# The last 16 of 256 tokens leave a dense expert product and are gathered instead

## The chip, the cores and the metric

The kernel runs on one core of a Trainium2 chip. The metric is the device time of one execution in microseconds. The engines are TensorE (PE; its loads of stationary operands are PEld), VectorE (DVE), ScalarE (ACT), GpSimd (POOL) and SyncE (SP), each with its own in-order queue of instructions; they wait for each other on semaphores.

## What is computed

Two transformer blocks over 256 tokens of width 1024. The change touches the last part only, a layer with 16384 experts (PEER), cut here to what matters:

```python
def peer(h, w_q, subkeys, w_down, w_up):            # h: 256 x 1024
    q = (h @ w_q)                                   # 8 heads, two halves of 128
    s = einsum('btphd,phnd->btphn', q, subkeys)     # 128 scores for each half
    v, i = top_k(s, 16)
    cand = v[..., 0, :, None] + v[..., 1, None, :]  # 16 x 16 pairs
    cidx = i[..., 0, :, None] * 128 + i[..., 1, None, :]
    tv, tj = top_k(cand, 16)                        # 16 experts a token and head
    eidx = take_along_axis(cidx, tj)
    w = softmax(tv)
    a = gelu(einsum('btd,btpkd->btpk', h, w_down[eidx]))
    return einsum('btpk,btpkd->btd', w * a, w_up[eidx])
```

So each token uses 128 of the 16384 rows of w_down.

## The kernel before

It does not gather. It computes the down products of all experts densely, multiplies their gelu by a matrix of routing weights that is zero where an expert is not chosen, and multiplies by w_up. The experts are cut into 128 tiles (NE) of 128 experts; expert number is i * 128 + j, a tile has one j. A tile is [128 experts x 256 tokens]; WA[:, j, :] holds it.

All weights come as one stream of pieces of 128 x 1024 float32 (512 KB), issued by SP into three ring slots. Each piece q is split into a high part of type fp32r by ScalarE (split_high, L192) and a low part, the remainder, by VectorE or GpSimd (split_low, L199), three pieces ahead of TensorE (AHEAD). The ring slot is free once the low part is made. A product of two such pairs is three matmuls, high-high, low-high, high-low (mm3, L273, L274, L277). In the wide form (down_wide, L2337 and L2341) the token operand's two parts lie side by side, so that a matmul of 512 columns does two of the three, one of 256 the third; ScalarE copies the right half out (L2355) and VectorE adds it (L2357).

The stage runs in this order.

Query pieces: 16 pieces, scores, and the top 16 of each half on VectorE (L2427 to L2434).

Lead tiles 0 to 35 (FIRST = 36), by lead_tile(u): the plain product, the split of the piece three ahead with the low part on GpSimd, the gelu on ScalarE (L2365). Beside them VectorE does the second top 16 (L2466 to L2473), the decoding of its places (to L2497), four picks of indices (L2510 to L2514, twice for each half of the tokens) and the softmax (L2516 to L2525; Exp on ScalarE, L2518, between tile 29 and 30). Tiles 6 to 29 are in a hardware loop (nc.Fori), the others are unrolled. Before tile 33, TensorE turns indices and weights (turn_route, L2532), before tile 35 come the first one-hot matrices.

64 steps g, one for each 4 tokens (TB, ROUTES): VectorE makes one-hot matrices of 4 tokens (onehots, L2557, L2558), ScalarE scales one by the weights (weights_in, L2566), TensorE multiplies them (route_product, L2575) and then does the wide tile 36 + g. The routing weights of these tokens go to WA by ScalarE's copy for tiles that have no gelu yet (route_copy, L2586) and by VectorE's multiplication for those that have (route_multiply, L2594). late_gelu (L2610, L2612) and late_weigh (L2623) weigh the part of the tile whose tokens' weights are already there. Each queue is in the written order: ScalarE in step g has weights_in(g+1), late_gelu(g-1), route_copy(g-1), the high part of the piece three ahead, the copy of the right half. VectorE has route_multiply(g-2), late_weigh(g-2), onehots(g+2), the low part, the addition.

Then 28 pairs of a wide down tile and an up tile (pair), then the remaining 100 up tiles (last_tile, last_up), and the end.

## Time and profile before

| | us |
|---|---|
| median of 3 runs | 1719.74 |
| lowest, highest | 1718.23, 1723.38 |
| span of the profiled execution | 1718.3 |
| TensorE busy | 1692.9 |
| VectorE busy | 1283.4 |
| ScalarE busy | 970.7 |
| GpSimd busy | 234.7 |

Times in the rows are in microseconds from the start of the span. A line of a timeline gives start, duration, engine, line, operation, output and input; several instructions that follow each other can be merged into one with a count. Durations of neighbouring instructions of one engine overlap, so the distance between starts is what one costs. The words in square brackets are the idle time of the engine before it and who ended it. "Share" of DMA is the mean busy share of the 16 DMA engines. PEclk is TensorE's granted clock as a share of 2.4 GHz.

In the execution profiled, the lead tiles take 943 to 1046 us in all, with the last query scores among the first three; the 64 steps run to 1281, the pairs to 1437, the up tiles to 1701.

### The profile page before, as it was taken

What the parts mean: (1) busy time and instruction counts of PE and PEld (TensorE: products, weight loads), DVE (VectorE), ACT (ScalarE), POOL (GpSimd) and SP (SyncE); (2) the same over time, 40 slices, a digit from 0 to 9 for tenths busy, and PEclk for the clock granted to TensorE, in tenths of its full rate; (3) what the DMA queues carried; (4) which work ended last, traced back from release to release, by engine and by line L of the source; (5) the groups of instructions that cost most, each with busy time, mean ns of one, the idle gap of its engine ahead of it and who ended that gap; (6) DMA issues with size and microseconds to landing.
All of it is one profiled execution on the core that took longest, in us unless ns stands there. A gap on an engine that the chain in (4) does not pass through costs nothing.

```text
span 1718.3 us, 30152 instructions
## 1 busy us (share of the span) xinstructions
PE 1692.9 (99%) x10170; PEld 1497.8 (87%) x10170; DVE 1283.4 (75%) x2549; ACT 970.7 (56%) x1798; POOL 234.7 (14%) x172
## 2 busy tenths in 40 slices
PE   9999999999999999999899999999999999999998
PEld 8888888799888887889899999999988888888886
DVE  5468877867788788867658766889987666666667
ACT  5746554566555544557455548988874544333333
POOL 2120000011100000321117883000000000000000
PEclk9999999999999999999999999999999999999999
DMA  7535767655547686444245555444446555555554
GB/s 243 189 127 156 267 206 281 212 176 202 207 146 268 217 284 243 165 160 140 82 138 170 178 180 169 140 143 148 140 143 193 187 194 185 194 195 193 190 192 146
DMA packets 86579, 317.50 MB, mean 185 GB/s; under 512 B 9664, under 2 KB 9936, under 8 KB 85968
## 3 DMA queue, kind: packets, MB, share of 16 engines
q1 hardware_dynamic: 77328, 279.48, 49.2%
q10 hardware_dynamic: 7200, 25.45, 4.0%
q0 software_dynamic: 1952, 11.25, 1.9%
q8 instruction: 61, 1.00, 0.2%
q14 instruction: 38, 0.31, 0.1%
HBM read 315.08 MB, written 1.05 MB: 184 GB/s over the span
## 4 chain that ended last, share of the span: by engine, by line
PE 69%; DVE 4%; ACT 2%; DMA 2%; issue 1%; POOL 0%; DVEq 0%; SPq 0%; ACTq 0%
PE bank L273 13%; PE bank L277 13%; PE bank L274 13%; PE bank L2337 10%; PE bank L2341 5%; PE bank L1250 4%; PE bank L2575 3%; PE bank L1254 2%; DVE wl L199 1%; DMA ada<-in_w_ada 1%; ACT wh L192 1%; PE bank L622 1%; DMA ring<-in_stream 1%; PE bank L676 1%; PE bank L699 1%
## 5 line engine op out<-in xcount | busy, mean ns | idle before, releaser
L192 ACT ACTIVATE wh<-ring 128x1024 fp32r<-128x1024 f32 x526 | 555.6, 1058 | 537.6 <-PE bank L277 356.1
L199 DVE TENSOR_TENSOR wl<-ring,wh 128x1024 fp32r<-128x1024 f32 x468 | 572.8, 1226 | 279.2 <-ACT wh L192 277.8
L273 PE MATMUL bank<-wh,xs 128*128 128x512 f32 (+1 forms) x780 | 279.5, 358 | 2.0 <-DVE wl L199 0.8
L277 PE MATMUL bank<-wh,xs 128*128 128x512 f32 (+1 forms) x780 | 275.7, 353 | 0.0
L274 PE MATMUL bank<-wl,xs 128*128 128x512 f32 (+1 forms) x780 | 275.4, 353 | 0.0
L2337 PE MATMUL bank<-xs,wh 128*128 128x512 f32 x736 | 250.8, 402 | 0.0
L1250 PE MATMUL bank<-xs,wh 128*128 128x512 f32 x672 | 212.4, 396 | 1.9 <-DVE wl L199 1.9
L273 PE MATMUL bank<-xs,wh 128*128 128x256 f32 x616 | 177.4, 288 | 0.3 <-ACT fox_v L1127 0.2
L277 PE MATMUL bank<-xs,wl 128*128 128x256 f32 x616 | 174.3, 283 | 0.0
L274 PE MATMUL bank<-xs,wh 128*128 128x256 f32 x616 | 174.2, 283 | 0.0
L199 POOL TENSOR_TENSOR wl<-ring,wh 128x1024 fp32r<-128x1024 f32 x57 | 138.4, 2430 | 262.0 <-ACT wh L192 168.4
L273 PEld LDWEIGHTS bank<-wh,xs 128*128 128x128 f32 x780 | 147.4, 189 | 25.5 <-DVE wl L199 2.9
L277 PEld LDWEIGHTS bank<-wh,xs 128*128 128x128 f32 x780 | 147.3, 189 | 20.7
L274 PEld LDWEIGHTS bank<-wl,xs 128*128 128x128 f32 x780 | 147.5, 189 | 20.3 <-issue 0.5
L2341 PEld LDWEIGHTS bank<-xs,wl 128*128 128x128 f32 x736 | 138.5, 188 | 29.3
L1254 PEld LDWEIGHTS bank<-xs,wl 128*128 128x128 f32 x672 | 126.2, 188 | 29.5
L2341 PE MATMUL bank<-xs,wl 128*128 128x256 f32 x736 | 145.1, 279 | 0.0
L1254 PE MATMUL bank<-xs,wl 128*128 128x256 f32 x672 | 132.1, 278 | 0.0
L2337 PEld LDWEIGHTS bank<-xs,wh 128*128 128x128 f32 x736 | 119.1, 189 | 1.1
L273 PEld LDWEIGHTS bank<-xs,wh 128*128 128x128 f32 x616 | 118.1, 192 | 0.8 <-ACT fox_v L1127 0.4
L274 PEld LDWEIGHTS bank<-xs,wh 128*128 128x128 f32 x616 | 118.1, 192 | 0.1
L277 PEld LDWEIGHTS bank<-xs,wl 128*128 128x128 f32 x616 | 117.9, 191 | 0.0
(505 smaller groups left out, 2849.6 us busy)
## 6 DMA issues: line engine op xcount, KB each, us to landing
ring<-in_stream SPq DMA_DIRECT2D x529, 512.0 KB, 3.4
ada<-in_w_ada ACTq DMA_DIRECT2D x48, 512.0 KB, 4.7
rows<-in_rows POOLq DMA_DIRECT2D x1, 2560.0 KB, 11.3
rows<-in_rows POOLq DMA_DIRECT2D x3, 512.0 KB, 5.2
con<-in_early POOLq DMA_DIRECT2D x1, 1374.0 KB, 14.4
x_feature_major<-in_x_fm SPq DMA_DIRECT2D x4, 256.0 KB, 5.9
x<-in_x_tm POOLq DMA_DIRECT2D x1, 1024.0 KB, 5.5
rows<-in_rows POOLq DMA_DIRECT2D x1, 1024.0 KB, 7.5
```

Source lines behind the costliest of these rows:

```text
L192: C.activation(wh[q % AHEAD][:, :], ring[slot][:, :], ACT.Copy).then_inc(s_high, 1)
L199: low.tensor_tensor(wl[q % AHEAD][:, :], ring[slot][:, :], wh[q % AHEAD][:, :], ALU.subtract).then_inc(s_low, 1)
L273: T.matmul(o, left[0], right[0], start=start, stop=False, skip_group_check=True)
L274: T.matmul(o, left[0], right[1], start=False, stop=False, skip_group_check=True)
L277: return T.matmul(o, left[1], right[0], start=False, stop=stop, skip_group_check=True)
L622: T.matmul(o, v[0], w[:, 0:S], start=first, stop=False, skip_group_check=True)
L676: scored = pe.did(T.matmul(b[:, P:3 * P], q[:, P:2 * P], k, start=True, stop=True, skip_group_check=True))
L1250: return T.matmul(g[:, :], h[:, ks], xs[:, k, :, :].rearrange("p a t -> p (a t)"), start=k == 0, stop=stop, skip_group_check=True)
L1254: return T.matmul(g[:, 0:S], l[:, ks], xh[:, k, :], start=False, stop=stop, skip_group_check=True)
L2337: return T.matmul(b[:, :], h[:, ks], xs[:, k, :, :].rearrange("p a t -> p (a t)"), start=k == 0, stop=stop, skip_group_check=True)
L2341: return T.matmul(b[:, 0:S], l[:, ks], xh[:, k, :], start=False, stop=stop, skip_group_check=True)
L2575: last = T.matmul(bank[g % 4][:, k * P:(k + 1) * P], oh_i[g % 2][:, k, :], oh_j[g % 2][:, k, :], start=True, stop=True, skip_group_check=True)
```

## The change

The last 16 tokens (TAKEN) are left out of all down products: every down matmul takes 240 columns (LIVE) instead of 256, or two runs of 240 instead of 512; copies, additions and gelus of down tiles shrink likewise. For these tokens, VectorE sums the high and low part of their activations (own_copies), TensorE turns them so that the 128 partitions are 8 heads x 16 tokens (own_rows). After the picks of the second half of the tokens, which now come first, VectorE works out their expert numbers; ScalarE issues eight small transfers that lay them out one per partition (choose); GpSimd issues 16 indirect transfers, one for each of the 16 choices, which bring 128 rows of w_down of 4 KB each to ten buffers (gather); VectorE multiplies each with the own rows and sums (chosen_dot). The dots go through eight more small transfers (dots_by_token), a gelu and a transposition, and multiply the routing weights of these tokens (chosen_weights). Their route_multiply becomes a copy. The up products still have all 256 tokens.

FIRST goes from 36 to 45, so 45 plain tiles lead, 64 wide ones are in the steps and 19 in the pairs. The loop has tiles 6 to 23. From tile 28 on (BY_POOL) the low parts in the lead are VectorE's. The difference and the Exp of the softmax come before the picks, the rest of it (route_weights) after tile 29.

```diff
-FIRST = 36
+FIRST = 45
 TB = 4
+TAKEN = 16
+LIVE = S - TAKEN
+BY_POOL = 28
...
+    rows_of = [carve(D) for i in range(10)]
+    own = carve(D)
+    picks_of = carve(PH * TOPK, dt=I32)
...
-                last = mm3(bank[4 + u % 3][:, 0:S], (h[:, k * P:(k + 1) * P], l[:, k * P:(k + 1) * P]),
-                           (xh[:, k, :], xl[:, k, :]), k == 0, k == KD - 1)
+                last = mm3(bank[4 + u % 3][:, 0:LIVE], (h[:, k * P:(k + 1) * P], l[:, k * P:(k + 1) * P]),
+                           (xh[:, k, 0:LIVE], xl[:, k, 0:LIVE]), k == 0, k == KD - 1)
...
+                    return T.matmul(sides, h[:, ks], xs[:, k, :, 0:LIVE], start=k == 0, stop=stop, skip_group_check=True)
+                    return T.matmul(b[:, 0:LIVE], l[:, ks], xh[:, k, 0:LIVE], start=False, stop=stop, skip_group_check=True)
...
+    def lead_tile(u, i, low=G):
         n = 0 if i is None else i * BODY
         down(q0 + u, n, u, n, first=i is None and u < 3)
-        split(q0 + u + AHEAD, i, low=G)
+        split(q0 + u + AHEAD, i, low=low)
...
+    def own_copies():
+
+        parts_of = [part[:, :, LIVE:S].unsqueeze(2).broadcast_to([P, KD, PH, TAKEN]) for part in (xh, xl)]
+        return dve.did(V.tensor_tensor(own_f, parts_of[0], parts_of[1], ALU.add))
+
+    def own_rows(ready):
+
+        pe.wait(ready, moved[2 * PH - 2])
+        for k in range(KD):
+            dst = bank[1 if k < 4 else 7][:, k % 4 * P:(k % 4 + 1) * P]
+            last = T.matmul(dst, rows_of[0][:, k * P:(k + 1) * P], ident, start=True, stop=True, skip_group_check=True)
+        made = pe.did(last)
+        act.wait(made)
+        C.activation(own[:, 0:HALF], bank[1], ACT.Copy)
+        return act.did(C.activation(own[:, HALF:D], bank[7], ACT.Copy))
+
+    dve.wait(operand["high"][KD - 1], operand["low"][KD - 1])
+    own_ready = own_copies()
...
+            if ph == 2 * PH + 1:
+                own_done = own_rows(own_ready)
...
+    LOOPED = BY_POOL // BODY * BODY
+    with nc.Fori(1, LOOPED // BODY, engines=(ENG.PE, ENG.Activation, ENG.Pool)) as i:
...
-    for w in range(2):
-        for t in range(NT):
+    for t in (1, 0):
+        for w in range(2):
...
+        if t == 1:
+            dve.wait(picked)
+            numbered = dve.did(V.scalar_tensor_tensor(picks_of, IJ[:, 0, 1].rearrange("p h k -> p (h k)"), float(NE),
+                                                      IJ[:, 1, 1].rearrange("p h k -> p (h k)"), ALU.mult, ALU.add))
+
+    def choose():
+
+        act.wait(numbered)
+        for h in range(PH):
+            C.dma_start(chosen[h * TAKEN:(h + 1) * TAKEN, :],
+                        picks_of[P - TAKEN:P, h * TOPK:(h + 1) * TOPK]).then_inc(s_chosen, 16)
+
+    def gather(r):
+
+        if r == 0:
+            G.wait_ge(s_chosen, 16 * PH)
+        if r >= len(rows_of):
+            G.wait_ge(s_dot, r - len(rows_of) + 1)
+        G.indirect_dma_start(rows_of[r % 10], None, a["down_rows"],
+                             bass.IndirectOffsetOnAxis(ap=chosen[:, r:r + 1], axis=0)).then_inc(s_row[r % 10], 16)
+
+    def chosen_dot(r):
+
+        row = rows_of[r % 10]
+        dve.wait(own_done)
+        V.wait_ge(s_row[r % 10], 16 * (r // 10 + 1))
+        V.tensor_tensor_reduce(out=row, in0=row, in1=own, scale=1.0, scalar=0.0, op0=ALU.mult, op1=ALU.add,
+                               accum_out=dots[:, r:r + 1]).then_inc(s_dot, 1)
+
+    def dots_by_token():
+
+        C.wait_ge(s_dot, TOPK)
+        for h in range(PH):
+            C.dma_start(dots_t[:, h * TOPK:(h + 1) * TOPK], dots[h * TAKEN:(h + 1) * TAKEN, :]).then_inc(s_dots_t, 16)
+
+    def chosen_gelu():
+
+        C.wait_ge(s_dots_t, 16 * PH)
+        return act.did(C.activation(dots_t[:, :], dots_t[:, :], ACT.Gelu_apprx_tanh))
...
+        if g == 0:
+            C.wait_ge(s_dot, TOPK)
...
+        if TB * g >= LIVE:
+            V.tensor_copy(dst, by_tile(g)[:, 0:hi, :]).then_inc(s_wm, 1)
+            return
...
+    choose()
+    for u in range(LOOPED, BY_POOL):
+        lead_tile(u, None)
+        for r in range(2 * (u - LOOPED), 2 * (u - LOOPED) + 2):
+            gather(r)
+    for r in range(2 * (BY_POOL - LOOPED), TOPK):
+        gather(r)
+    V.wait_ge(s_low, q0 + BY_POOL + AHEAD)
+    for u in range(BY_POOL, FIRST):
         if u == FIRST - 3:
             i_in = turn_route(0, IJ[:, 0], picked, iT)
             j_in = turn_route(1, IJ[:, 1], picked, jT)
@@ -2632,13 +2737,18 @@
         if u == FIRST - 1:
             onehots(0)
             weights_in(0)
-        lead_tile(u, None)
+        lead_tile(u, None, low=V)
+        if u == BY_POOL + 1:
+            wd = route_weights()
+        if u >= FIRST - TOPK:
+            chosen_dot(u - (FIRST - TOPK))
     onehots(1)
-    V.wait_ge(s_low, q1 + AHEAD)
     for g in range(ROUTES - 1):
         route_product(g)
         down_wide(q1 + g, 0, FIRST + g, 0)
         if g + 1 < ROUTES:
+            if TB * (g + 1) == LIVE:
+                act.wait(weighed_in)
             weights_in(g + 1)
         if g >= 1:
             late_gelu(g - 1)
@@ -2652,6 +2762,14 @@
             onehots(g + 2)
         split(q1 + g + AHEAD)
         late_whole(g)
+        if g == 2:
+            dots_by_token()
+        if g == 5:
+            chosen_ready = chosen_gelu()
+        if g == 8:
+            chosen_turned = chosen_turn(chosen_ready)
+        if g == 10:
+            weighed_in = chosen_weights(chosen_turned, w_in)
```

## Rows read from the trace of the kernel before

**Rows 1.** The page: TensorE's busy time and the chain that ended last.

```profile
PE 1692.9 (99%) x10170; PEld 1497.8 (87%) x10170; DVE 1283.4 (75%) x2549; ACT 970.7 (56%) x1798; POOL 234.7 (14%) x172
...
PE 69%; DVE 4%; ACT 2%; DMA 2%; issue 1%; POOL 0%; DVEq 0%; SPq 0%; ACTq 0%
```

**Rows 2.** Windows, lead tiles: us busy by engine; last PEclk, DMA share, GB/s.

```profile
953.00:1046.00 93.00, 93.00 (x778) 93.00 (x777) 64.31 (x185) 48.58 (x76) 77.25 (x33) 1.00 0.55 177
```

**Rows 3.** Timeline of TensorE in a lead tile.

```profile
1000.11 0.28 PE L273 MATMUL bank<-xs,wh 128*128 128x256 f32 x1
1000.23 0.28 PE L274 MATMUL bank<-xs,wh 128*128 128x256 f32 x1
```

**Rows 4.** Timeline of TensorE in a step of the late tiles.

```profile
1101.11 0.39 PE L2337 MATMUL bank<-xs,wh 128*128 128x512 f32 x1
1101.34 1.05 PE L2575 MATMUL bank<-onehot_j,onehot_i 128*128 128x128 f32 x8
1102.15 0.48 PE L2337 MATMUL bank<-xs,wh 128*128 128x512 f32 x1
```

**Rows 5.** Timeline of TensorE: short moving operands and plain f32.

```profile
376.36 0.60 PE L676 MATMUL bank<-foxk_T,foxq_T 65*128 65x256 f32 x2
...
801.59 1.42 PE L1965 MATMUL bank<-kc_pair,nqT 128*128 128x30 f32 x12
```

**Rows 6.** Timeline of ScalarE at tile 29, the last of the loop.

```profile
1028.39 1.06 ACT L192 ACTIVATE wh<-ring 128x1024 fp32r<-128x1024 f32 x1 [1.55 <-PE bank L277]
...
1029.74 1.28 ACT L2518 ACT_TABLE_LOAD   x1
1031.03 0.42 ACT L2518 ACTIVATE weighted<-weighted 128x256 f32<-128x256 f32 x1
```

**Rows 7.** Timeline of GpSimd in the lead.

```profile
1003.61 2.40 POOL L199 TENSOR_TENSOR wl<-ring,wh 128x1024 fp32r<-128x1024 f32 x1 [0.48 <-ACT wh L192]
```

**Rows 8.** Timelines of ScalarE's queue and of GpSimd: issues that follow each other.

```profile
11.04 0.39 ACTq L143 DMA_DIRECT2D keep<-in_keep  x1
...
11.47 0.45 ACTq L143 DMA_DIRECT2D vec<-in_vec  x1
...
76.56 0.53 POOL L143 DMA_DIRECT2D rows<-in_rows  x1
```

**Rows 9.** Timeline of VectorE: candidates, first pick, reduction of the last pick.

```profile
961.19 1.42 DVE L2460 TENSOR_TENSOR weighted<-bank,weighted 128x256 f32<-128x256 f32 x4 [5.00 <-ACT bank L2441]
...
989.31 2.30 DVE L2510 TENSOR_TENSOR bank<-bank,keep 128x2048 f32<-128x2048 f32 x1
...
1014.95 2.29 DVE L2514 TENSOR_REDUCE weighted<-bank 128x128 f32<-128x2048 f32 x1
```

**Rows 10.** Timeline of VectorE: a product with sum, a one-hot, a low part.

```profile
389.06 1.22 DVE L384 CUSTOM_DVE_ANT_0 ada<-ada,silu_c 128x1024 f32<-128x1024 f32 x1
...
1274.83 0.68 DVE L2558 TENSOR_TENSOR onehot_j<-keep,route_j 128x512 f32<-128x512 f32 x1
1275.65 1.23 DVE L199 TENSOR_TENSOR wl<-ring,wh 128x1024 fp32r<-128x1024 f32 x1
```

**Rows 11.** Timeline of ScalarE in a late step.

```profile
1062.35 1.27 ACT L2566 ACTIVATE onehot_j<-onehot_j,route_w 128x128 f32<-128x128 f32 x4
...
1064.22 0.45 ACT L2586 ACTIVATE weighted<-bank 128x352 f32<-128x352 f32 x1
1064.80 1.06 ACT L192 ACTIVATE wh<-ring 128x1024 fp32r<-128x1024 f32 x1
```

**Rows 12.** DMA issues of 350 to 500 us: KB each, median us to landing.

```profile
ada<-in_w_ada ACTq DMA_DIRECT2D x12, 512.0 KB, 4.3
```

**Rows 13.** Timeline of TensorE and a window: idle time, then the granted clock.

```profile
849.76 0.52 PE L699 MATMUL bank<-keep,ss_p 128*128 128x128 f32 x3 [2.45 <-POOL ss_p L666]
...
852.00:854.00 2.00, 2.00 (x8) 1.82 (x9) 2.00 (x8) 0.28 (x1) 0.94 (x1) 0.50 0.16 59
```

**Rows 14.** Timeline of VectorE beside GpSimd's low part.

```profile
1039.07 2.11 DVE L2557 TENSOR_TENSOR onehot_i<-keep,route_i 128x512 f32<-128x512 f32 x1 [6.35 <-ACT route_j L2535]
```

## What the change does to the time: a prediction

> **What bounds the kernel now.** I read the page first: TensorE is busy for 99% of the span, and the chain of work that ended last is TensorE for 69%, with small shares elsewhere [rows 1]. Then the stretch of the lead tiles by windows: TensorE has no idle time in it, VectorE is busy for 64 of 93 us, GpSimd for 77 [rows 2]. So in the part of the program that the change touches, every microsecond goes through TensorE, and two questions decide: how much shorter its instructions become, and whether the other engines still deliver in time.
>
> TensorE's busy time is of no use for the first, since its instructions overlap; distances between starts are. In a lead tile one starts every 0.12 us (1000.11, 1000.23) with 256 columns [rows 3]; with 512 columns the next starts 0.23 us later (1101.11 to 1101.34) [rows 4]. At the granted 2.4 GHz that is N columns plus 32 in both cases: (256+32)/2.4 = 120 ns, (512+32)/2.4 = 227 ns. A lead tile is 24 of them, 2.88 us. A wide tile has 8 of 512 and 8 of 256 columns, 2.77 us, and four routing products take 1101.34 to 1102.15 plus what the next instruction waits, about 0.91; together 3.68 a step.
>
> **The columns taken away.** 16 columns at 2.4 GHz are 6.67 ns. A lead tile saves 24 x 6.67 = 0.16 us (pitch 113 ns, tile 2.72). A wide tile loses 32 columns in 8 instructions and 16 in 8 others, again 0.16 us. All 128 tiles: **20.5 us**. That an instruction can go down to 113 ns: twelve products with only 30 moving columns stand in 1.42 us, (1.42 - 0.27)/11 = 0.105 us each [rows 5], so loading 128 stationary columns does not hold one above some 0.11 us. The other end is that the lead stays at 120 ns because something of the load adds to it: then 45 x 0.16 = 7.2 us of the gain are gone. I take 113, since 512 and 256 columns lie on one line. The moving operand of the wide tiles becomes two runs of 240; no row shows two runs, I take nothing, and up to 5 us (8 x 83 instructions, 8 ns each) for the range.
>
> The Trainium skill (TensorE: Matmul & The Clock Gate, section LDWEIGHTS) gives the load of a stationary operand as columns / 1.2 GHz, 107 ns for 128. If the 13 ns that each instruction carries here came on top of the load as they do on top of the columns, 240 columns would still start every 120 ns; by that rule the lead gains nothing and the sum below would be 7.2 us worse. Rows 5 speak for a bound nearer 0.11 us.
>
> **Work added on TensorE.** The own rows of the 16 tokens: 8 products in plain f32, each recorded as two instructions; the eight instructions of rows 4 take 0.11 us each, so 16 x 0.11 = 1.8 us, in the lead, where nothing hides them. The late transposition is one such product, 0.2 us. The copies of these (two of 512 elements on ScalarE) and the VectorE sum of 1024 elements fall into idle time. FIRST from 36 to 45 moves nine tiles from wide to plain; both have 24 x 256 columns, so it is worth nothing by itself. **+2.0 us.**
>
> **ScalarE before tile 24.** Write T(u) for the release at the end of tile u. Today ScalarE does the high half (1.06) and the gelu, and idles 1.55 of 2.88 us [rows 6]. The loop now ends with tile 23. Behind it stand: high half and gelu 1.35, the table load for Exp 1.28, then the eight issues of choose(), then the high half of piece 27. Two issues on ScalarE's queue stand 0.43 us apart (11.04, 11.47) [rows 8]: 8 x 0.43 = 3.4. (Their indices are there: VectorE's chain begins its picks at 989.31 and has done two of the four, 7 us each, by 1004 plus 1 [rows 9], while T(23) falls at about 1009: T(29) at 1028.39 [rows 6], less six tiles of 2.88, plus 1.8 for the own rows, less some 3.) So piece 27 is ready at T(23) + 1.35 + 1.28 + 3.4 + 1.06 + 2.40 (GpSimd's low half [rows 7]) + 0.2 = 9.7, and TensorE wants it after three tiles, 8.2: **+1.6 us.** If issues cost only the 0.34 us for which ScalarE's later ones are busy, it is 0.8.
>
> **GpSimd in tiles 24 to 27.** The low halves of pieces 28, 29 and 30 now have two gathers before each. A low half is 2.40 in a tile of 2.72, so 0.32 is free. The trace has no indirect transfer; a direct one of 128 rows holds GpSimd for 0.53 us [rows 8], which is the lower end (less is not to be had, as the indices have to be read too); the upper is its one long operation, 2.4 us. I take 1.0, twice the direct one, nearer to it since both write 128 descriptors. Each of three tiles then waits 2 x 1.0 + 2.40 - 2.72 = 1.7: **+5.0 us** (ends: 2.2 and 13). Queued behind the gathers are these low halves only; from piece 31 on VectorE makes them at 1.23 instead of 2.40, with slack.
>
> **VectorE at the end of the lead.** It has per tile a low half (1.23) and, from tile 29, a dot over 1024 elements; the same operation on ada takes 1.22 [rows 10]. 2.45 fits in 2.72. But onehots(0) stands behind the low half of piece 46 and dot 14, which wait for T(43): high half to +1.1, low half +2.3, dot +3.5, two one-hots of 0.62 each to +4.8, and ScalarE scales them in 1.3 [rows 11], +6.1. TensorE wants them for the first routing product at T(44) = +2.7: **+3.4 us.** ScalarE stood in that wait, so the high half of piece 47 comes at +7.1, its low half +8.3, dot 15 +9.5, onehots(1) +10.8, scaled +12.1; TensorE has its next tile done at 6.1 + 0.9 + 2.6 = 9.6: **+2.5 us.** In the kernel before the one-hots stood in VectorE's idle time. If the dots are overlapped better than rows 10 say, 2 us less.
>
> **ScalarE in step 2 of the late tiles.** Its copy ends at 1064.67 and TensorE releases it at 1064.80 [rows 11]: it has 0.13 us a step to spare before, and by the shorter copies (328 instead of 364 elements) about nothing after. dots_by_token() puts eight issues, 3.4 us, after the high half and behind them the scaling for product 4: T(2) + 1.0 + 3.4 + 1.3 = 5.7 against a step of 3.52: **+2.2 us.** The rest of the late stage keeps its 0.16: ScalarE's step shrinks with the tile number, and VectorE, whose step at 1274 leaves 0.14 us of 3.68, gets the bound only in the last few.
>
> **Transfers.** Sixteen gathers are 8.4 MB more, ten of them issued within some 15 us, beside a stream that has 177 GB/s at a share of 0.55 [rows 2]. Where the ada rows came beside the stream, they landed in 4.3 us [rows 12] and TensorE did not wait. The ring allows a landing of about 5.5 us from tile 28 on; I take 1.0 us in all, bounds 0 and 5. **The clock**: after a gap of 2.45 us the granted clock was 0.50, 1.2 GHz, in the window behind [rows 13]. The wait of 3.4 us at the first product may do the same; if the next tile then runs at half rate (3.5 us for wide tile and product more), 2.5 of them lie in the wait that follows: I take **+0.9**.
>
> **Sum**: -20.5 + 2.0 + 1.6 + 5.0 + 3.4 + 2.5 + 2.2 + 1.0 + 0.9 = -1.9 us on the profiled span of 1718.3. That span is 1.4 us under the median of the runs shown, 1719.74, whose lowest is 1718.23; applied to the median: **1717.8 us**.
>
> What lies next to the gathers: a one-hot on VectorE beside GpSimd's low half took 2.11 us instead of 0.68 [rows 14, 10]. The Trainium skill (SBUF — State Buffer, section SBUF: two separate sides) says that GpSimd and a VectorE operation with two SBUF inputs exclude each other for a whole instruction. The row agrees. By that rule the gathers from tile 28 on and VectorE's low halves and dots hold each other up; eight gathers of 1 us in 17 tiles would use up the 0.27 us per tile that VectorE has free and add up to 3 us at the first product.
>
> **The rivals.**
> Waits smaller than I say (0.29): issues at 0.34 or hidden behind running work, gathers at 0.53 us, no clock loss. Then 2.0 + 0.8 + 2.2 + 3.4 + 2.5 + 1.5 = 12.4 of cost, net -8.1: 1711.6. For it: TensorE's columns are certain, the waits are built from single rows. Against: the order of the queues is in the code, and two of the waits do not hang on unknown prices.
> The low halves held up by the gathers (0.17), the one that ends slower: from 1.9 us a gather on, the three tiles lose 3 x (3.8 - 0.3) = 10.5 instead of 5.0, and with transfers of 2 us more the net is +5.6: 1725.3. It decides from g = 1.8 us. For it: nothing else of GpSimd's was ever paced this tightly (0.48 idle a tile).
> The 240 columns gain nothing in the lead (0.12): -1.9 + 7.2: 1725.0 at the worst, 1721.4 at half.
> The change doesn't do what it says (0.04): columns below 256 lose the fast rate. A plain f32 product of 256 columns starts its next 0.22 us later [rows 5] and needs two instructions; at that price the 24 x 45 + 8 x 83 narrow instructions cost some 0.29 us more each, +500 us, about 2200. No row has fewer than 256 columns at this type, which is all that speaks for it.
> The forecast itself has 0.38.
>
> **How the numbers follow.** Range 1708 to 1728: below it reaches past 1711 for cheaper dots, above to the gathers and the lead without gain, and leaves the last rival out. 0.3% is 5.2 us, about what a measurement of this kernel tells from no change. Faster by more (under 1714.6): the first rival, 0.25 of its 0.29, and 0.09 of the forecast's own spread, 0.34. Slower (over 1724.9): 0.11 of the second, 0.07 of the third and the whole of the fourth, 0.22. Between: 0.44.
>
> **What would show it.** Starts 113 ns apart in the lead, 2.72 us a tile; a step of the late tiles of 3.52. TensorE waiting for GpSimd's low half in tiles 27 to 30, for ScalarE's scaled one-hot at the first two products and at the fifth. GpSimd's indirect issues at 1.0 us; ScalarE's eight issues at 3.4 us. Wrong would be: pitch 120 in the lead; no idle TensorE at the first product; a stream that lands later than 5.5 us with TensorE waiting for VectorE's low halves between tiles 31 and 43.

## The result, and the profile after

Median **1725.67 us** (five runs, 1723.46 to 1726.36) against 1719.74 us before (five runs beside it, 1718.23 to 1723.38): 1.0029 times as long, 95% interval 1.0015 to 1.0042. The change costs about 5 us where I forecast a gain of 1.9. The profiled execution took 1723.82 us with a span of 1722.5, 4.2 us more than the span before; the accounts below are made on these two spans.

The page: TensorE is a point less busy than in [rows 1], the chain now has VectorE in it for 9% and TensorE for 62%.

```profile
PE 1683.0 (98%) x10259; PEld 1497.7 (87%) x10259; DVE 1303.4 (76%) x2574; ACT 964.3 (56%) x1789; POOL 232.4 (13%) x180
...
PE 62%; DVE 9%; ACT 4%; issue 2%; DMA 1%; POOL 1%; ACTq 0%; DVEq 0%; SPq 0%
```

The columns first. Timeline of TensorE in a lead tile; it answers to [rows 3]:

```profile
999.74 0.28 PE L278 MATMUL bank<-xs,wh 128*128 128x240 f32 x1
999.85 0.27 PE L281 MATMUL bank<-xs,wl 128*128 128x240 f32 x1
999.96 0.27 PE L277 MATMUL bank<-xs,wh 128*128 128x240 f32 x1
1000.07 0.27 PE L278 MATMUL bank<-xs,wh 128*128 128x240 f32 x1
```

The starts are 0.11 us apart; 24 of them are a tile, and the distance between the ends of undisturbed tiles is 2.68 us (111.7 ns each) where it was 2.88. A late step went from 3.68 to 3.53, the down half of a pair from 2.78 to 2.64. With 33 lead tiles at -0.20, the first three at -0.19, 64 late steps at -0.15, 19 pairs at -0.14, and nine tiles that were the down half of a pair before (2.78) and are lead tiles now (2.68), this is some 20.3 us. The gain came in full.

What ate it are waits that TensorE did not have. The waits of TensorE by releaser, 1014 to 1122 us (us in total, times, longest):

```profile
PE bank L2666 <- ACT onehot_j L2657: 6.9, 3, 3.4
PE bank L277 <- POOL wl L203: 3.6, 3, 1.8
PE bank L277 <- ACT weighted L2379: 2.0, 1, 2.0
PE bank L277 <- DVE wl L203: 1.8, 3, 0.8
```

These 14.3 us are idle time alone; the distances between tile ends, which hold half-clock work too, tell the whole. Over the undisturbed pitch they show: 1.8 at tile 2 (own rows); 1.8 at tile 27; 2.2, 3.7 and 0.5 at tiles 28, 29 and 30; 0.3, 0.9, 0.5 and 1.0 at tiles 33, 35, 36 and 37; 5.3 and 0.8 at the first two routing products; 4.8 at product 4; 0.4 for the late transposition at product 9. That is 24.0.

**ScalarE's issues**, timeline around product 4 (ACTq is ScalarE's queue of issues):

```profile
1092.13 1.06 ACT L196 ACTIVATE wh<-ring 128x1024 fp32r<-128x1024 f32 x1
1092.18 1.16 ACTq L2587 DMA_DIRECT2D chosen_dots_by_token<-chosen_dots  x2
1093.10 0.35 ACT L2369 ACTIVATE gelu<-bank 128x240 f32<-128x240 f32 x1
1093.37 3.81 ACTq L2587 DMA_DIRECT2D chosen_dots_by_token<-chosen_dots  x6
1097.23 1.28 ACT L2657 ACTIVATE onehot_j<-onehot_j,route_w 128x128 f32<-128x128 f32 x4 [3.78 <-DVE onehot_j L2649]
```

The first two overlap ScalarE's running instructions, the other six take 0.64 us each with nothing beside them, and the one-hots stand behind. The releaser in brackets, VectorE, had been done before (its last one-hot ended at 1096.29). What TensorE loses there, its timeline and the windows behind (columns as under VectorE below):

```profile
1098.56 1.47 PE L2666 MATMUL bank<-onehot_j,onehot_i 128*128 128x128 f32 x8 [2.99 <-ACT onehot_j L2657]
```

```profile
1098.00:1100.00 2.00, 1.44 (x9) 1.45 (x10) 0.00 (x0) 2.00 (x6) 0.81 0.00 0
1100.00:1102.00 2.00, 2.00 (x9) 1.79 (x8) 1.81 (x5) 1.81 (x7) 0.50 0.00 0
1102.00:1104.00 2.00, 2.00 (x12) 1.76 (x11) 1.27 (x3) 0.58 (x3) 0.83 0.70 221
```

Only 3.0 of the 4.8 us are idle time. At tiles 27 and 28, where the clock stayed at 1.00 (1015 to 1025 us), a wait cost about 0.25 us more than its idle time (1.77 for 1.54, 2.22 for 1.97). By that, an estimate, some 3.2 us of product 4's loss are the wait and some 1.6 the lower clock behind it.

**GpSimd**, timeline at tiles 28 to 30:

```profile
1019.44 2.37 POOL L203 TENSOR_TENSOR wl<-ring,wh 128x1024 fp32r<-128x1024 f32 x1
1021.97 0.95 POOL L2572 DMA_INDIRECT weighted<-in_down_rows,chosen_rows  x1 [0.16 <-issue]
1023.23 0.94 POOL L2572 DMA_INDIRECT weighted<-in_down_rows,chosen_rows  x1 [0.30 <-issue]
1024.19 2.36 POOL L203 TENSOR_TENSOR wl<-ring,wh 128x1024 fp32r<-128x1024 f32 x1
```

From low half to low half it is 4.75 us, TensorE's tile is 2.68. (The wait at tile 28, 2.0 us, ends by the record with a gelu on ScalarE at 1021.88, behind a high half that had waited 2.0 us for its piece; GpSimd's low half ended at 1021.81, so there the two were late together.) At tile 29 the clock comes on top. TensorE's wait there, and two windows behind it (PE, PEld, DVE, ACT, POOL; clock, DMA share, GB/s):

```profile
1026.70 0.35 PE L277 MATMUL bank<-xs,wh 128*128 128x240 f32 x1 [1.81 <-POOL wl L203]
```

```profile
1027.00:1029.00 2.00, 2.00 (x14) 2.00 (x13) 0.00 (x0) 0.38 (x2) 1.67 (x3) 0.64 0.83 279
1029.00:1031.00 2.00, 2.00 (x11) 2.00 (x10) 0.00 (x0) 0.00 (x0) 2.00 (x1) 0.51 1.02 317
```

**VectorE before the first product**, timeline, and windows of the same stretch (busy us of PE, PEld, DVE, ACT, then granted clock, DMA share, GB/s):

```profile
1073.89 1.23 DVE L203 TENSOR_TENSOR wl<-ring,wh 128x1024 fp32r<-128x1024 f32 x1 [0.20 <-ACT wh L196]
1075.03 1.22 DVE L2580 CUSTOM_DVE_ANT_0 weighted<-weighted 128x1024 f32<-128x1024 f32 x1
...
1076.18 0.68 DVE L2648 TENSOR_TENSOR onehot_i<-keep,route_i 128x512 f32<-128x512 f32 x1
1076.78 0.68 DVE L2649 TENSOR_TENSOR onehot_j<-keep,route_j 128x512 f32<-128x512 f32 x1
```

```profile
1075.00:1077.00 2.00, 0.39 (x4) 0.19 (x2) 2.00 (x5) 0.00 (x0) 1.00 0.60 193
1077.00:1079.00 2.00, 0.17 (x1) 0.17 (x2) 0.46 (x1) 1.50 (x5) 0.94 0.46 168
1079.00:1081.00 2.00, 2.00 (x9) 2.00 (x10) 1.25 (x2) 0.97 (x2) 0.50 0.01 4
1081.00:1083.00 2.00, 2.00 (x10) 1.77 (x10) 2.00 (x4) 0.00 (x0) 0.71 0.41 111
```

Low half, dot, one-hots, as the forecast had them. TensorE idles, and when it starts again the granted clock is 0.50 (1.2 GHz) and then 0.71: it is "busy" for 4 us and starts some 20 products.

### The profile page after: what moved, and what is told of

The parts are those of the page before. It is cut to its first block, busy times and chain, and to the rows that moved or that the text cites. A ratio compares the mean times of both kernels' runs of the same rounds, so it can differ in the third digit from the quotient of the medians.

```text
span 1722.5 us, 30270 instructions
## 1 busy us (share of the span) xinstructions
PE 1683.0 (98%) x10259; PEld 1497.7 (87%) x10259; DVE 1303.4 (76%) x2574; ACT 964.3 (56%) x1789; POOL 232.4 (13%) x180
## 4 chain that ended last, share of the span: by engine, by line
PE 62%; DVE 9%; ACT 4%; issue 2%; DMA 1%; POOL 1%; ACTq 0%; DVEq 0%; SPq 0%
PE bank L277 13%; PE bank L281 13%; PE bank L278 13%; PE bank L2352 8%; PE bank L2355 4%; PE bank L2666 3%; DVE wl L203 3%; PE bank L1254 2%; ACT wh L196 2%; DMA ring<-in_stream 1%; PE bank L1258 1%; PE bank L626 1%; PE bank L680 1%; PE bank L703 0%; POOL wl L203 0%
## 5 line engine op out<-in xcount | busy, mean ns | idle before, releaser
L277 PE MATMUL bank<-wh,xs 128*128 128x512 f32 (+1 forms) x816 | 293.7, 360 | 1.9 <-DVE wl L203 0.9
L281 PE MATMUL bank<-wh,xs 128*128 128x512 f32 (+1 forms) x816 | 289.8, 355 | 0.0
L278 PE MATMUL bank<-wl,xs 128*128 128x512 f32 (+1 forms) x816 | 289.6, 355 | 0.0
L2352 PE MATMUL bank<-xs,wh 128*128 128x480 f32 x664 | 219.8, 392 | 0.0
L1254 PE MATMUL bank<-xs,wh 128*128 128x512 f32 x672 | 212.6, 396 | 2.4 <-DVE wl L203 2.4
L277 PE MATMUL bank<-xs,wh 128*128 128x240 f32 (+1 forms) x688 | 196.0, 285 | 7.6 <-POOL wl L203 3.6
L278 PE MATMUL bank<-xs,wh 128*128 128x240 f32 (+1 forms) x688 | 192.2, 279 | 0.0
L281 PE MATMUL bank<-xs,wl 128*128 128x240 f32 (+1 forms) x688 | 192.2, 279 | 0.0
L203 POOL TENSOR_TENSOR wl<-ring,wh 128x1024 fp32r<-128x1024 f32 x49 | 117.6, 2403 | 255.4 <-ACT wh L196 163.6
L277 PEld LDWEIGHTS bank<-xs,wh 128*128 128x128 f32 x688 | 131.8, 192 | 9.4 <-issue 4.8
L1258 PE MATMUL bank<-xs,wl 128*128 128x256 f32 x672 | 132.2, 278 | 0.0
L278 PEld LDWEIGHTS bank<-xs,wh 128*128 128x128 f32 x688 | 131.8, 192 | 0.1
L2355 PE MATMUL bank<-xs,wl 128*128 128x240 f32 x664 | 128.4, 275 | 0.0
L2352 PEld LDWEIGHTS bank<-xs,wh 128*128 128x128 f32 x664 | 108.0, 192 | 0.8
```

Source lines behind the costliest of these rows:

```text
L203: low.tensor_tensor(wl[q % AHEAD][:, :], ring[slot][:, :], wh[q % AHEAD][:, :], ALU.subtract).then_inc(s_low, 1)
L277: T.matmul(o, left[0], right[0], start=start, stop=False, skip_group_check=True)
L278: T.matmul(o, left[0], right[1], start=False, stop=False, skip_group_check=True)
L281: return T.matmul(o, left[1], right[0], start=False, stop=stop, skip_group_check=True)
L1254: return T.matmul(g[:, :], h[:, ks], xs[:, k, :, :].rearrange("p a t -> p (a t)"), start=k == 0, stop=stop, skip_group_check=True)
L1258: return T.matmul(g[:, 0:S], l[:, ks], xh[:, k, :], start=False, stop=stop, skip_group_check=True)
```

## Experiments

All are timed against the kernel before on the same chip; its medians there were 1719.99 to 1720.41 us. The numbers in brackets are the 95% interval of the ratio, about 0.1% or 1.7 us either way; so a difference of two medians of under some 3 us shows nothing by itself, and the distances between tile ends in the traces decide. Products are counted from 0: the first two are 0 and 1.

**1. The columns alone.** The kernel before with `LIVE = 240` in the products:

```diff
-  last = mm3(bank[4 + u % 3][:, 0:S], ..., (xh[:, k, :], xl[:, k, :]), ...)
+  last = mm3(bank[4 + u % 3][:, 0:LIVE], ..., (xh[:, k, 0:LIVE], xl[:, k, 0:LIVE]), ...)
```

and the same for the two products of a wide tile.

> The kernel before with its expert down products over 240 columns instead of 256 and nothing else of the change (left out: the last 16 tokens get no fresh down products, so their part of the output is not computed). Theory (the columns gain what I forecast, and the loss is all in the added steps): lead tile 2.88 to 2.68 us (33 tiles, 6.6), first three 3.32 to 3.13 (0.6), late step 3.68 to 3.53 (64, 9.6), pair's down half 2.78 to 2.64 (28, 3.9), 20.7 in all; the changed kernel showed 2.785 instead of 2.724 us for the up half of a pair, and if that belongs to the columns 28 of them give back 1.7: 19.0 faster than before, 1700.7 us. Rival A (the dearer up half comes from something else of the change, such as where the lead ends): the up half stays at 2.724 and the time is 1699.0. Rival B (part of the changed kernel's loss lies in the shorter products themselves, by a lower clock or by lows that come too late for the shorter pitch): under 15 us faster, with waits of TensorE on the low halves in the lead.

Measured: 1700.10 us, 0.9889 (0.9872 to 0.9905), 20.1 less than before. Lead tile 2.68, late step 3.53, pair's down half 2.64, no new wait. So the columns are worth what I said, and the whole loss lies in the added work. The up half of a pair went from 2.72 to 2.75: half of what the changed kernel's 2.785 has more than 2.724 comes with the columns; where the other half comes from stays open. Together it is 19 x 0.06 = 1.2 us.

**2. Fewer columns still** (`LIVE = 224`).

> The kernel before with its expert down products over 224 columns (left out: the last 32 tokens' down products). It measures how the pitch goes on below 240. If the pitch of a product goes by its columns, as from 256 (120 ns) to 240 (111.7 ns), a lead tile goes from 2.68 to 2.52 or less and a late step from 3.53 to about 3.38: some 36 us faster than before. If something other than the columns sets it from about 240 down, such as the load of the weights, a lead tile stays near 2.68 and the time falls by only about 22 to 30 us, and the up half of a pair gets dearer again.

Measured: 1690.70 us, 0.9829 (0.9813 to 0.9846). The late step fell to 3.41 and the pair's down half to 2.52, the lead tile not at all, 2.68. Timeline of TensorE in its lead:

```profile
999.81 0.27 PE L274 MATMUL bank<-xs,wh 128*128 128x224 f32 x1
999.92 0.27 PE L275 MATMUL bank<-xs,wh 128*128 128x224 f32 x1
1000.03 0.28 PE L278 MATMUL bank<-xs,wl 128*128 128x224 f32 x1
```

0.11 us again: in the lead 240 columns are at a floor that 224 do not pass. Taking 16 more tokens out would pay only in the wide tiles.

**3. No gathers.**

```diff
         lead_tile(u, None)
-        for r in range(2 * (u - LOOPED), 2 * (u - LOOPED) + 2):
-            gather(r)
-    for r in range(2 * (BY_POOL - LOOPED), TOPK):
-        gather(r)
+    G.wait_ge(s_chosen, 16 * PH)
```

and the dots multiply the own rows with themselves, without a wait for a landing.

> The changed kernel without its sixteen gathers; the dots multiply own rows with themselves (left out: the routed down rows of the last 16 tokens, so their output is wrong). Theory: the waits of TensorE at tiles 28 to 30 (6.4 us, the clock drop to 0.51 at 1029 us among them) and the late stream pieces at tiles 33 to 37 (2.8) both come from the gathers, and go: 9.2 faster than the changed kernel, 1716.5 us, and the first routing product's wait shrinks too if VectorE had been held back by those. Rival A: the waits at tiles 28 to 30 are the low halves on GpSimd beside VectorE's selection, whatever stands between them: they stay above 3 us. Rival B: tiles 33 to 37 wait for VectorE (low half and dot a tile), not for the stream: 2.8 stays.

Measured: 1716.15 us, 0.9975 (0.9966 to 0.9985), 9.5 less than the changed kernel; expected 9.2. Tiles 28 to 41 all end 2.69 us apart, so both rivals fall (on the two profiled spans the gain is 5.5: this execution came to the lead 2.7 us later and lost 1.1 more at product 4). ScalarE's high halves show what the gathers had done to the stream, 1014 to 1060 us (idle time and what ended it), the changed kernel and this one:

```profile
L196 ACT ACTIVATE wh<-ring 128x1024 fp32r<-128x1024 f32 x15 | 15.9, 1061 | 29.1 <-DMA ring<-in_stream 26.2 <-PE bank L281 2.8
```

```profile
L196 ACT ACTIVATE wh<-ring 128x1024 fp32r<-128x1024 f32 x17 | 18.0, 1061 | 21.8 <-PE bank L281 14.8 <-DMA ring<-in_stream 7.0
```

Nearly all of its idle time ends with a landing in the first, a third in the second. The first two products lost 3.7 and 2.3 us here, 6.0 together, and product 4 lost 6.0: those do not come from the gathers. Tile 27 still lost 1.4.

**4. Gathers behind the last low half of GpSimd.**

```diff
         lead_tile(u, None)
-        for r in range(2 * (u - LOOPED), 2 * (u - LOOPED) + 2):
-            gather(r)
-    for r in range(2 * (BY_POOL - LOOPED), TOPK):
+    for r in range(TOPK):
         gather(r)
```

> The changed kernel with all sixteen gathers behind GpSimd's last low half instead of two behind each of the last four. If the instruction time of the gathers on GpSimd is what TensorE waits for at tiles 28 to 30, those 6.4 us go (little is left, under 1). But the first gather is issued some 2 to 5 us later, the first dots wait for landings of 7 us, and each waiting dot holds a low half behind it on VectorE: I expect 2 to 5 us of new waits around tiles 30 to 34, and the stream's pieces late as before, so 1721 to 1724. The rival (it is the traffic, not GpSimd's time) has waits of 5 us or more stay at the tiles in which the gathers run, 1725 or more.

Measured: 1724.32 us, 1.0023 (1.0009 to 1.0037). Tiles 28 to 30 lose nothing. The edit moves the gathers' traffic away from there too, but tiles 29 and 30 waited for low halves 4.75 us apart with GpSimd busy between them, so there it was GpSimd's instruction time. But 5.3 us come back at tiles 33 to 43, waits for VectorE, and the first product is 7.4 late instead of 5.3. Only the place of the wait was moved.

**5. The dots turned by GpSimd's queue.**

```diff
-        C.wait_ge(s_dot, TOPK)
+        G.wait_ge(s_dot, TOPK)
         for h in range(PH):
-            C.dma_start(dots_t[...], dots[...]).then_inc(s_dots_t, 16)
+            G.dma_start(dots_t[...], dots[...]).then_inc(s_dots_t, 16)
```

> The changed kernel with the eight transfers that turn the dots by token issued by GpSimd, which has nothing to do by then, instead of ScalarE. If the 4.85 us that TensorE waits before product 4 are the 5.0 us of ScalarE's eight issues, that step comes back to 3.53 and the time falls by about 4.9 us, to 1720.8. The rival (ScalarE is late there for other reasons: the copy of product 0 waits for the last dot, and the weighing of the one-hots stands behind it): the wait shrinks to no less than 2 us, and the time falls by under 3.

Measured: 1721.91 us, 1.0002 (0.9993 to 1.0012), 3.8 less than the changed kernel. Step 4 ends 3.53 us after step 3: the wait is gone and the clock loss behind it, and the issues were the cause of both.

**6. One-hots a tile earlier, with ScalarE's weighing.**

```diff
-        if u == FIRST - 1:
+        if u == FIRST - 2:
             onehots(0)
             weights_in(0)
```

and `onehots(1)` ahead of dot 15.

> The changed kernel with the one-hots of products 0 and 1 put ahead of dots 14 and 15 on VectorE, one tile earlier each. If TensorE waits for the first two products because the one-hots stand behind a low half and a dot each, most of the 6.05 us go (5.3 and 0.8), the clock drop at 1080 us with them: about 1720. Against it: VectorE has a low half and a dot for nearly every tile and is behind by then; in that case the wait moves to the low halves of pieces 46 and 47 or to ScalarE's copy of product 0, which waits for the last dot, and the gain is under 3 us. The wait before product 4 stays or grows.

Measured: 1725.49 us, 1.0029 (1.0019 to 1.0039): nothing. The first product now loses 1.3 us, the second 6.3. I had moved ScalarE's weighing ahead of the high half of piece 46, so that piece stood behind the one-hots in its place. The ten runs spread from 1719.98 to 1728.94.

**7. Both (5 and 6).**

> Both of these together. If the two causes are apart the gains add: 4.9 and 6 us, to about 1715. If ScalarE's issues only filled a time in which it waited for the last dot anyway, the sum is well under that: the copy of product 0 still waits for dot 15, and 1717 or more is measured.

Measured: 1719.67 us, 1.0001 (0.9992 to 1.0011), 6.0 less than the changed kernel; product 4's wait is gone, the second product still loses 4.8. Not the sum I had hoped for, since edit 6 alone had moved its wait instead of removing it.

**8. Four edits, low halves of tiles 37 to 44 back on GpSimd.** Edits 4, 5 and 6 and, with `BACK = 37` and two waits at the changes of engine,

```diff
-        lead_tile(u, None, low=V)
+        lead_tile(u, None, low=V if u < BACK else G)
```

> Four edits together: the two above, the sixteen gathers behind GpSimd's last low half (25 to 28 us of gathers in a row), and GpSimd takes the low halves of tiles 37 to 44 back, so that VectorE has only dots there. Adding up from the trace of the changed kernel: 4.9 (issues), 6.0 (first two products) and 6.4 less 0.9 for what choosing still costs (tiles 28 to 30) go, the stream's late pieces stay (2.8 to 5, as the run with the gathers last showed 6 us of waits at tiles 33 to 42): 1709 to 1714 us, faster than both kernels. The rival: the gathers end only at about 1047 us, the dots follow them at 1.2 to 2.7 us each, and the last dot comes later than the first product, so that a wait of 2 to 5 us for ScalarE's copy of product 0 takes their place: 1715 to 1719.

Measured: 1719.34 us, 0.9994 (0.9985 to 1.0003). I missed this one: tiles 33 to 39 lost some 4.5 us, the first and the third product 1.1 and 2.3, and tile 40 alone 5.5. Timelines of VectorE and GpSimd there, and TensorE's wait:

```profile
1063.20 3.39 DVE L2580 CUSTOM_DVE_ANT_0 weighted<-weighted 128x1024 f32<-128x1024 f32 x1
...
1066.52 3.39 DVE L2580 CUSTOM_DVE_ANT_0 weighted<-weighted 128x1024 f32<-128x1024 f32 x1
```

```profile
1059.06 9.77 POOL L203 TENSOR_TENSOR wl<-ring,wh 128x1024 fp32r<-128x1024 f32 x3 [4.85 <-ACT wh L196]
```

```profile
1062.34 0.54 PE L277 MATMUL bank<-xs,wh 128*128 128x240 f32 x1 [2.72 <-POOL wl L203]
```

A dot that takes 1.22 us alone takes 3.39 beside a low half on GpSimd, and the low half 3.26 instead of 2.4: they take turns. The Trainium skill (SBUF — State Buffer, section SBUF: two separate sides) has a VectorE operation with two SBUF inputs and a GpSimd operation that reads SBUF exclude each other for a whole instruction; the rows agree. Giving VectorE's low halves to GpSimd relieves nobody while the dots run. But taking turns made that low half only 0.9 us longer. It began late too, at 1059.06, because its piece had come late (ScalarE idled 2.3 us for it), and behind TensorE's 2.7 us of idle time the granted clock was 0.64 and then 0.50 from 1061 to 1067 us, which is most of the other half of the 5.5.

**9. More room: a lead of 48 tiles** (`FIRST = 48`), so that the dots lie three tiles later.

> The changed kernel with a lead of 48 tiles instead of 45, nothing else: the sixteen dots lie in tiles 32 to 47 instead of 29 to 44, so VectorE has three tiles with a low half alone between GpSimd's last low half and the first dot. Theory (TensorE waits for the first two routing products because VectorE, with a low half and a dot of 1.14 us each in every tile of 2.68 us and held up by late pieces and rows, is behind by then; moving the one-hots within its queue did not help for that reason): with 4.6 us more room the 6.05 us of these two waits and the clock drop behind them shrink to under 1.5, and the time falls by some 5 us, to about 1720.5. The rival (the order at the end sets it, a low half and a dot ahead of the one-hots, as I counted in the forecast: 3.4 and 2.5 us): the waits stay near 5.9 us and the time near 1725.6.

Measured: 1725.43 us, 1.0034 (1.0022 to 1.0046): no gain. The first two products lose 5.2 and 0.9 us as before, so the rival holds: VectorE is not behind, the order is what counts.

**10. The same with the dots turned by GpSimd.**

> The same with the eight transfers that turn the dots issued by GpSimd. By the earlier run with that edit alone product 4's wait (4.85 us) goes: 4.9 less than the run with the longer lead alone, about 1715.6 if the theory there holds, 1720.7 if the rival does.

Measured: 1720.95 us, 1.0003 (0.9991 to 1.0014), the rival's number; product 4 on time. The profiled execution (span 1721.7) is no faster than that of the run before (1721.4): it reached the lead 1.3 us later, lost 2.5 more in tiles 27 to 44, and its first product came 7.4 us late.

**11. One gather per tile.** All gathers behind the low halves, and ahead of each

```diff
+        G.wait_ge(s_used, q0 + BY_POOL + r + 1)
         gather(r)
```

> The same once more, with all gathers behind GpSimd's last low half and held to one per tile of TensorE, from tile 28 on, so that the dot of each comes four tiles behind its gather. Theory: the 6.4 us of waits at tiles 28 to 30 go, because no gather stands between low halves, and the late stream pieces (2.8 us) too, because the two kinds of transfers no longer ask for more than 512 KB each per 2.68 us: about 9 us less than the run before, 1706 to 1707. The rival: even one gather of 512 KB a tile beside the stream delays pieces (380 GB/s together, against some 370 at most in the changed kernel's windows), so 3 to 6 us of waits stay in tiles 31 to 45: 1709 to 1712.

Measured: 1715.29 us, 0.9974 (0.9965 to 0.9984), 5.7 less than without the pacing (8.4 on the profiled spans, 1721.7 and 1713.3). Tiles 28 to 44 all end 2.69 us apart: no wait in the whole stretch, where the run before lost some 10 us. Windows 1036 to 1056 us (PE, PEld, DVE, ACT, POOL; clock, DMA share, GB/s), the changed kernel and this one:

```profile
1036.00:1056.00 20.00, 18.19 (x156) 17.53 (x155) 15.95 (x24) 8.13 (x13) 8.81 (x7) 1.00 1.02 404
```

```profile
1036.00:1056.00 20.00, 20.00 (x181) 20.00 (x180) 15.11 (x20) 9.06 (x14) 7.13 (x8) 1.00 1.02 402
```

Both move some 400 GB/s at a share of 1.02. One gather and one piece a tile, 2 x 512 KiB in 2.68 us, are 391 GB/s: paced, they just fit in this execution. The first product is 7.3 us late here, as in the run before (7.4). Timeline of ScalarE:

```profile
1071.73 1.06 ACT L196 ACTIVATE wh<-ring 128x1024 fp32r<-128x1024 f32 x1 [2.20 <-DMA ring<-in_stream]
```

A late piece: the copies of the turned routes stand behind this high half and hold low half 48 up, and two low halves and two dots stand ahead of the one-hots. So part of what the transfers cost is paid here.

**12. ScalarE's first eight issues spread**, two ahead of each of tiles 24 to 27:

```diff
-    choose()
+    act.wait(numbered)
     for u in range(LOOPED, BY_POOL):
+        choose(2 * (u - LOOPED))
         lead_tile(u, None)
```

> The same with ScalarE's eight issues for the chosen rows spread over tiles 24 to 27, two a tile, instead of all ahead of tile 24's instructions: the wait at tile 27 (1.8 us) should go, 1705. If that wait is GpSimd's low half beside VectorE's last selection steps and not ScalarE's issues (without the gathers it was still 1.4), it stays.

Measured: 1712.99 us, 0.9961 (0.9947 to 0.9975). The medians differ by less than they can tell, but tile 27 loses nothing: those issues were its cause. Tiles 37 and 40 lost 0.8 and 1.4 in this execution, in which 1036 to 1056 us moved only 360 GB/s at a share of 0.99, under the 391 that the pacing asks for. At the limit of the transfers it is not always quiet, and no run tells what sets the rate.

**13. The order of the one-hots alone**, on the changed kernel:

```diff
             dve.wait(i_in, j_in)
+            onehots(0)
             act.wait(w_in)
         if u == FIRST - 1:
-            onehots(0)
+            onehots(1)
             weights_in(0)
```

> The changed kernel with the one-hots of product 0 on VectorE right behind the turned routes (tile 42), ahead of low half 45 and dot 13, those of product 1 ahead of low half 47, and ScalarE's weighing left where it was, behind the high half of piece 46. Theory (order alone): the waits at the first two products, 5.28 and 0.77 us, fall to under 1 together, the clock drop at 1080 us goes with them; product 4's wait (4.85) stays: about 1720.2. The rival (VectorE has too much to do in tiles 29 to 44, whatever the order): what the one-hots gain, low halves 45 to 47 lose, and at most 2 us are saved, 1723.7 or more.

Measured: 1720.56 us, 1.0002 (0.9993 to 1.0011), 5.1 less than the changed kernel. The first two products lose 0.2 and 0.6 us, and the clock stays up (windows as above, GpSimd's column added):

```profile
1075.00:1077.00 2.00, 2.00 (x17) 1.83 (x16) 2.00 (x2) 1.79 (x4) 0.00 (x0) 1.00 0.71 244
1077.00:1079.00 2.00, 2.00 (x15) 1.82 (x13) 2.00 (x5) 0.65 (x3) 0.00 (x0) 1.00 0.80 262
```

So it was not the idea of experiment 6 that failed. This edit differs from it in ScalarE's order, and also puts the one-hots still earlier on VectorE; which of the two made the difference no run tells apart.

**14. All that helped** (lead of 48, 5, 11, 12 and 13).

> The run with the lead of 48 tiles, paced gathers, GpSimd's issues and the spread issues of ScalarE, and this order of the one-hots too. Its first product came 7.06 us late and its second 0.63, with the clock at 0.50 from 1076 to 1082 us. By the theory nearly all of that goes (0.3 left): 1706, faster than the kernel before by 14 us. By the rival 2 us go: 1711.

Measured: **1708.51 us**, 0.9931 (0.9918 to 0.9944) of the kernel before: 11.5 faster than it, 17.2 faster than the changed one. Waits of TensorE from 1012 to 1130 us:

```profile
PE bank L277 <- DVE wl L203: 3.9, 4, 1.3
PE bank L2665 <- ACT onehot_j L2656: 2.2, 2, 1.3
```

The 2.2 us at the products and the 3.9 at late low halves keep it from the 1706 expected (1036 to 1056 us moved 349 GB/s in this execution). Product 4 and tiles 27 to 36 lose nothing. b240, with none of the added work, is at 1700.1.

## Why the prediction was wrong, step by step

- **Columns, -20.5: right** (-20.3 from the distances, -20.1 measured alone). Their make-up was not, and that the total came out is partly luck: lead tiles gained 0.20 each instead of 0.16, late steps 0.15, pairs 0.14; and the nine tiles that became plain, which the forecast put at nothing, lost 0.1 each, as its own 2.88 and 2.77 us a tile say. "N columns plus 32" put 240 columns at 113 ns and they start every 111.7; 224 columns do so too, so this is a floor of the lead and no longer that line. The Trainium skill (TensorE: Matmul & The Clock Gate, section LDWEIGHTS) has 107 ns for the load; the floor is 5 ns over it. That 13 ns come on top of the load, by which the lead would have stayed at 120 ns, is refuted. Two runs of 240 columns in one product cost at most some 0.02 us a tile (2.64 where that line gives 2.61). The dearer up halves, **+1.2**, were not in the sum.
- **Own rows and late transposition, +2.0: right** (1.8 and 0.4).
- **ScalarE before tile 24, +1.6: right in size** (1.8), and experiment 12 confirms the cause. The issues cost more than my 0.43 each but began earlier, under ScalarE's running instructions; two errors that cancel.
- **GpSimd in tiles 24 to 27, +5.0: 6.4.** A gather holds GpSimd for 0.95 us as estimated, but 0.16 to 0.30 us of issue stand before each; I had left out this gap. With it a low half comes every 4.75 us, and 3 x (4.75 - 2.68) is 6.2. Tiles 28 and 29 waited 2.0 and 1.8 us (idle time); tile 30 hardly did, since tile 29 itself took longer, at a granted clock of 0.64 and 0.51 from 1027 to 1031 us. So the clock cost next to nothing here: TensorE would have waited for GpSimd in that time.
- **The first two products, +3.4, +2.5, clock +0.9: 6.8 against 6.1, right as a whole.** The first wait idled TensorE for 3.4 us as forecast, the clock fell as [rows 13] let one expect, and it cost some 1.6 (an estimate as at product 4) instead of 0.9; but the slow tile then hid most of the second wait (0.5 of idle time instead of 2.5). Experiment 3 gave 3.7 and 2.3 without any gather, so the up to 3 us that gathers and VectorE holding each other up might have added here did not come; experiment 13 proved the order to be the cause, experiment 9 refuted the story of a VectorE that cannot keep up.
- **ScalarE in step 2, +2.2: the worst miss, 4.8.** The queue that TensorE waits for was right. Two things in the term failed. The issue's price was taken from two issues at the start of the program, 0.43 us [rows 8]; here two took 0.58 and six in a row 0.64 each, eight together 5.0 us (1092.18 to 1097.18) instead of 3.4. As they began under the high half, this makes the wait some 3.2 instead of 2.2. And the clock behind this wait was put at nothing, though the wait forecast was near the 2.45 us of [rows 13]: it was 0.50 from 1100 to 1102 us and cost some 1.6, with no other wait to hide it.
- **Transfers, +1.0: 2.8.** I compared a landing of 4.3 us beside another stream [rows 12] with what the ring allows, and did not add up the rates: ten gathers of 512 KB were issued within 19 us (1017 to 1036), which with a stream piece every 2.68 us asks for some 470 GB/s, an estimate; 286 were moved in that time, with TensorE waiting, and 404 from 1036 to 1056, at a share of 1.02. The sign that the forecast named came: the stream landed after 6.4 us in the median (1014 to 1060) where it had allowed 5.5, and tiles 33 to 37 waited for VectorE's low halves.

Together on the spans: -20.3 + 1.2 + 1.8 + 0.4 + 1.8 + 6.4 + 6.1 + 4.8 + 2.8 = +5.0; up to the lead the profiled execution was 0.6 us ahead of that of before by chance, which leaves the 4.2 of the spans (with rounding). Against the forecast, -1.9, the difference is 2.6 from step 2 (1.0 by the longer wait for the issues, 1.6 by the clock), 1.8 from the transfers, 1.4 from GpSimd, 1.2 from the up halves, 0.6 from the columns, the own rows and tile 27, less 0.7 at the first products. So the step that failed is the sizing of the waits, in step 2 above all; the places of the waits were right, and none of the rivals came true. A net of 1.9 us out of a gain of 20.5 and 18.6 of losses is smaller than the error of such terms, and the sign of it was never safe. The nearest rival in size, gathers of 1.9 us and more (1725.3), came near 1725.67 by chance: the gathers ahead of the three low halves took 0.95.

## What to carry to other kernels

When work leaves the engine that bounds the kernel, its transfers still have to be issued by someone: count each issue as an instruction of the queue it stands in, at its price back to back, and put it where no one waits behind it. Add up the rates of the streams that overlap, and pace a burst to what they leave, rather than start it as early as it can. A wait of TensorE can cost more than its idle time by the clock behind it; count that at each wait, and ask whether the next wait hides it. And before giving a late engine more time, look at what stands ahead of the awaited instruction in its own queue: reordering won 5 us where three tiles more room won none.

## What the chip showed that I had not expected

- Six issues in a row on ScalarE's queue took 0.64 us each, the same eight on GpSimd 0.48 to 0.58.
- Products of 240 and of 224 columns start 0.11 us apart in the lead (2.68 us for 24), 256 columns 0.12.
- A gather of 128 rows of 4 KB held GpSimd for 0.94 us, 1.26 us from start to start, a few 1.9 to 2.0 us for a reason that no run tells; it landed after 7.3 us in the median (6.2, 7.3 and 7.6 in the three paced runs), a stream piece of the same size after 3.3 without them.
- From 1036 to 1056 us the runs with gathers moved 349 to 411 GB/s, all at a share of 0.96 to 1.02: a full share is not one rate. At 402 GB/s TensorE could still run without a wait for 17 tiles; at 349 and 360 the same pacing did not fit.
- Idle times of TensorE of 1.8, 2.7, 3.0 and 3.4 us were each followed, within 4 us of the restart, by a 2 us row with the granted clock at 0.50 or 0.51; the idle times of 1.5 and 2.0 us that stood 10 and 5 us before that 1.8 were not.
- A dot on VectorE beside GpSimd's low half: 3.39 us instead of 1.22.
